# Borders between the stages of a two-layer encoder: who adds the residual and splits the activations, and in what order the last gated-linear head finishes

## Chip, cores and metric

The kernel runs on one core of a Trainium2 chip. The metric is the device time of one execution, in microseconds (us); lower is better.

## What is computed

The reference runs 1024 prompt frames and 64 frames of a running stream (T = 1088 tokens together, D = 1024 channels, all in float32) through two layers:

```
layer 1: x += rms_norm(gated_linear_attention(rms_norm(x))) ; x += rms_norm(mlp(rms_norm(x)))
layer 2: x += rms_norm(sliding_window_attention(rms_norm(x))) ; x += rms_norm(mlp(rms_norm(x)))
rms_norm(x) = x / sqrt(mean(x * x) + 1e-6) * g        mlp(h) = relu(h @ w_up) ** 2 @ w_down
gated linear, per head, chunks of 64 frames: scores = (q decayed) @ (k decayed).T ; out = q @ state + scores @ v
        state = decay * state + k.T @ v ; out = rms_norm(out) * g * silu(r) ; result = out @ w_out
```

## The kernel before

**Layout.** Activations lie transposed: channels on the 128 partitions (eight tiles `k` or `m` of 128 channels), tokens along the free axis, in three blocks `b` of 384, 384 and 320 tokens. float32 accuracy comes from splitting each operand in a high and a low part: `h_hi`, `h_lo` for activations and `w_hi`, `w_lo` for weights, and three matmul passes (hi x hi, lo x hi, hi x lo).

**Weights.** They come in 180 units of 128 x 1024 values (512 KB) through four slots. SP's queue loads `w_raw`, ScalarE casts it to `w_hi` (`high` of the stream, L151), GpSimd subtracts and writes `w_lo` (L158), and TensorE's last matmul of a unit frees the slot. `dense` and `dense_set` (L181, L201) are the matmuls of a unit.

**Stages.** Gated linear (4 heads), MLP, attention, MLP. Each stage ends with a last wave, whose positions are (b, q): block b, output tile q, about one output tile of 12 to 24 matmuls each, and starts with a first wave, whose positions are (b, j): block b, output group j. Between two stages stands a `Border`; the program calls it five times (before the first stage, three in the middle, after the last). Its steps, for each block:

- the norm of the stage's output: `square` (ScalarE, L381) squares each tile, `add_squares` (VectorE, L463) adds it to an accumulator, `sums` (TensorE, L314) adds over partitions, `inverse` (VectorE and ScalarE's `root`) makes 1/sqrt and a diagonal (L512, L515), `spread` (TensorE, L323) spreads it over the partitions into a bank, and `scale` (VectorE, L524) multiplies the tiles `y`;
- the residual: `load_x` brings the old x from DRAM through four slots (`X_SLOTS`), `add_x` (L533) adds it;
- the next stage's input: `high` (ScalarE, L407) writes `h_hi` with the next norm's gain and squares x (L412), `low` (VectorE, L548) writes `h_lo`; `add_squares_x` (L477), `sums_x` (L333), `inverse_x`, `spread_x` (L340) and `keep_block` (ScalarE, L419) make that norm's factor, which is applied after the next stage's first matmuls, so the first wave doesn't wait for it before its results are taken.

The order on each engine is written out by hand: `tensor_in_last_wave`, `tensor_in_first_wave`, `scalar_...`, `vector_...` say at which position which step is issued. `step(b, s)` on VectorE issues `scale` of tile s with the steps that follow it for earlier tiles. Block 0 is normed within the last wave, block 1 around its end, block 2 in the first wave of the next stage. In the last border the same steps end in the output: `high` only asks for the next residual, and the tail is stored by SP.

**Gated linear.** Each head runs nine pairs p of chunks; a pair has three slots (`PARTS`), and a planner puts jobs (projections of the next head, for head 3 the first parts of the output projection) into `STEPS` slots, from which TensorE fills the time in which the pair's chain runs: turned key, scores (L1868), attention (VectorE, L2390), state update (L1906, L2415), output (L1922, L1925). `HIGHS` says at which slot ScalarE casts which weight unit. In head 3, `silu`, `early_high` (L2106) and `early_low` (L2313) prepare the gated outputs of earlier heads, `end_early` issues the four early jobs of the output projection, `gated` (L2299) finishes head 3's own outputs, and turn_rows (L1812) turns them.

## Time and profile before

| | |
|---|---|
| median of three executions | 2671.1 us (2668.15 to 2671.66) |
| the profiled execution | 2670.47 us, span 2668.7 us |
| mean granted TensorE clock | 0.971 of full speed |
| busy | TensorE 2531.0 us (95%), VectorE 967.9 (36%), ScalarE 822.0 (31%), GpSimd 445.0 (17%) |
| DMA | 139 MB, mean 52 GB/s |

The span is what the profiler covers of one execution; the execution's own time is 1.8 us more. Busy times are sums over the whole span, so they don't say where an engine waits. PE is TensorE, DVE VectorE, ACT ScalarE, POOL GpSimd, PEld TensorE's weight loads; L323 is line 323 of the kernel before. The granted clock is given in parts of full speed, 2.4 GHz.

### The profile page before, as it was taken

The page shows a single profiled execution, that of the slowest core. Times are in us where ns is not written, and L with a number is a line of the kernel's source. Part 1 is how long each engine was busy: PE and PEld are TensorE (multiplying, and loading weights), DVE is VectorE, ACT ScalarE, POOL GpSimd, SP SyncE. Part 2 cuts the span into 40 slices and gives each one's busy share as a digit, 9 for nine tenths or more (in the row PEclk, how much of TensorE's full clock was granted, in tenths as well). Part 3 has the DMA queues.
Part 4 walks back from the last instruction along what each step waited for, and adds up shares of the span by engine and source line. Part 5 has one row for each costly group of instructions (what it writes and reads, how often), then busy time and mean ns, then how long its engine had stood idle before and what let it go on. Part 6 is the DMA issues. An engine that isn't in the chain of part 4 may idle for free.

```text
span 2668.7 us, 41573 instructions
## 1 busy us (share of the span) xinstructions
PE 2531.0 (95%) x17454; PEld 2388.1 (89%) x17454; DVE 967.9 (36%) x1913; ACT 822.0 (31%) x1618; POOL 445.0 (17%) x186
## 2 busy tenths in 40 slices
PE   6999999898999999999998999889899999999997
PEld 5778878698999999999997977688899999999996
DVE  6354454416422222222228344425522222222227
ACT  4445444335311211120224355535411211211221
POOL 1101110111112211212211010112112212211210
PEclk9999999899999999999999999999999999999998
DMA  3101010013211111111113200103311111111113
GB/s 106 41 9 47 25 39 26 29 48 114 80 40 48 44 42 47 39 47 39 57 42 119 80 25 18 37 25 98 95 48 40 47 39 47 42 44 47 39 60 123
DMA packets 63088, 139.05 MB, mean 52 GB/s; under 512 B 8688, under 2 KB 39920, under 8 KB 62960
## 3 DMA queue, kind: packets, MB, share of 16 engines
q1 hardware_dynamic: 33984, 103.60, 12.0%
q10 hardware_dynamic: 28976, 33.64, 4.1%
q8 instruction: 93, 1.52, 0.2%
q14 instruction: 35, 0.29, 0.0%
HBM read 117.81 MB, written 19.40 MB: 51 GB/s over the span
## 4 chain that ended last, share of the span: by engine, by line
PE 77%; DVE 5%; issue 2%; ACT 2%; ACTq 0%; DMA 0%; DVEq 0%; SPq 0%
PE banks L201 51%; PE banks L181 19%; PE banks L1769 1%; DVE h_lo L548 1%; DVE norm_acc_x L477 1%; DVE norm_acc L463 1%; DVE y L524 1%; PE banks L1269 1%; PE banks L1288 1%; PE banks L323 0%; PE banks L1256 0%; PE banks L1296 0%; PE banks L1922 0%; PE banks L1925 0%; ACT y L1422 0%
## 5 line engine op out<-in xcount | busy, mean ns | idle before, releaser
L158 POOL TENSOR_TENSOR w_lo<-w_raw,w_hi 128x1024 fp32r<-128x1024 f32 x180 | 443.4, 2467 | 2151.3 <-ACT w_hi L151 2151.3
L181 PE MATMUL banks<-h_hi,w_hi 128*128 128x384 f32 (+1 forms) x1224 | 437.9, 358 | 8.1 <-POOL w_lo L158 5.3
L181 PE MATMUL banks<-h_lo,w_hi 128*128 128x384 f32 (+1 forms) x1224 | 415.9, 340 | 0.0
L181 PE MATMUL banks<-h_hi,w_lo 128*128 128x384 f32 (+1 forms) x1224 | 414.5, 339 | 0.0
L151 ACT CAST w_hi<-w_raw 128x1024 fp32r<-128x1024 f32 x180 | 187.0, 1047 | 468.0 <-DMA w_raw<-in_units 467.1
L201 PE MATMUL banks<-h_hi,w_hi 128*128 128x384 f32 (+1 forms) x1368 | 301.7, 329 | 0.0
L201 PE MATMUL banks<-h_hi,w_lo 128*128 128x384 f32 (+1 forms) x1368 | 301.3, 328 | 0.0
L201 PE MATMUL banks<-h_lo,w_hi 128*128 128x384 f32 (+1 forms) x1368 | 301.3, 328 | 0.0
L201 PE MATMUL banks<-mlp_a_hi,w_hi 128*128 128x384 f32 (+1 forms) x1344 | 296.6, 329 | 1.5 <-issue 1.3
L201 PE MATMUL banks<-mlp_a_lo,w_hi 128*128 128x384 f32 (+1 forms) x1344 | 295.1, 327 | 0.0
L201 PE MATMUL banks<-mlp_a_hi,w_lo 128*128 128x384 f32 (+1 forms) x1344 | 295.0, 327 | 0.0
L987 DVE TENSOR_TENSOR y<-banks,y 128x768 f32<-128x768 f32 x192 | 130.1, 719 | 401.6 <-PE banks L201 400.1
L916 ACT ACTIVATE mlp_act<-mlp_act 128x1088 f32<-128x1088 f32 x56 | 62.5, 1115 | 656.3 <-DVE mlp_act L973 656.3
L181 PEld LDWEIGHTS banks<-h_hi,w_hi 128*128 128x128 f32 x1224 | 241.5, 197 | 21.8 <-issue 19.0
L181 PEld LDWEIGHTS banks<-h_lo,w_hi 128*128 128x128 f32 x1224 | 241.8, 198 | 2.2 <-issue 0.6
L181 PEld LDWEIGHTS banks<-h_hi,w_lo 128*128 128x128 f32 x1224 | 240.9, 197 | 0.0
L973 DVE SCALAR_TENSOR_TENSOR mlp_act<-banks,keep 128x768 f32<-128x768 f32 x112 | 75.9, 720 | 444.5 <-PE banks L201 444.5
L201 PEld LDWEIGHTS banks<-h_hi,w_hi 128*128 128x128 f32 x1368 | 233.8, 188 | 0.0
L201 PEld LDWEIGHTS banks<-h_hi,w_lo 128*128 128x128 f32 x1368 | 233.8, 188 | 0.0
L201 PEld LDWEIGHTS banks<-h_lo,w_hi 128*128 128x128 f32 x1368 | 233.8, 188 | 0.0
L201 PEld LDWEIGHTS banks<-mlp_a_hi,w_hi 128*128 128x128 f32 x1344 | 226.7, 188 | 5.5 <-DVE y L987 3.1
L201 PEld LDWEIGHTS banks<-mlp_a_lo,w_hi 128*128 128x128 f32 x1344 | 227.3, 188 | 0.0
(191 smaller groups left out, 3108.3 us busy)
## 6 DMA issues: line engine op xcount, KB each, us to landing
w_raw<-in_units SPq DMA_DIRECT2D x180, 512.0 KB, 3.5
x_scratch<-y ACTq DMA_DIRECT2D x48, 192.0 KB, 2.5
norm_x<-x_scratch ACTq DMA_DIRECT2D x48, 192.0 KB, 3.3
x_scratch<-y ACTq DMA_DIRECT2D x24, 160.0 KB, 1.8
norm_x<-x_scratch ACTq DMA_DIRECT2D x24, 160.0 KB, 3.1
y<-in_x SPq DMA_DIRECT2D x16, 192.0 KB, 4.7
norm_x<-in_x ACTq DMA_DIRECT2D x16, 192.0 KB, 3.5
out_y<-y SPq DMA_DIRECT2D x16, 192.0 KB, 2.7
```

Source lines behind the costliest of these rows:

```text
L151: self.chip.nc.scalar.copy(self.chip.w_hi[:, s], self.chip.w_raw[:, s]).then_inc(self.hi_done, 1)
L158: c.nc.gpsimd.tensor_tensor(c.w_lo[:, s], c.w_raw[:, s], c.w_hi[:, s].bitcast(F32), ALU.subtract).then_inc(self.ready, 1)
L181: mm = chip.nc.tensor.matmul(out, w, x, start=(first and n == 0), stop=(last and n == 2))
L201: mm = chip.nc.tensor.matmul(chip.banks[:, 3 * s + b, 0:WIDTH[b]], w, x[:, k, COLS[b]], start=(k == 0 and n == 0), stop=(k == n_k - 1 and ...
L463: self.chip.nc.vector.tensor_tensor(self.s.acc[:, 0:n], before, self.s.sq[:, m % 2, 0:n], ALU.add).then_inc(self.s.summed, 1)
L477: self.chip.nc.vector.tensor_tensor(self.s.acc_x[:, 0:n], before, self.s.sq_x[:, k % 2, 0:n], ALU.add).then_inc(self.s.summed_x, 1)
L524: self.chip.nc.vector.scalar_tensor_tensor(out=y, in0=y, scalar=self.chip.gains[:, gain, k:k + 1], in1=self.chip.banks[:, RS_BANK + b % 2, ...
L548: op = nc.vector.scalar_tensor_tensor(out=lo, in0=y, scalar=self.chip.gains[:, self.pre, k:k + 1], in1=hi.bitcast(F32), op0=ALU.mult, op1= ...
L916: nc.scalar.activation(self.act[:, j % 2], self.act[:, j % 2], ACT.Square).then_inc(self.squared, 1)
L973: op = nc.vector.scalar_tensor_tensor(out=out, in0=bank, scalar=0.0, in1=keep, op0=ALU.max, op1=ALU.mult)
L987: op = nc.vector.tensor_tensor(y, bank, y, ALU.add)
L1269: nc.tensor.transpose(out[:, 0:P], prob[:, 1:1 + P], chip.ident[:])
```

## The change

At the middle borders and the last one:

- ScalarE's squares go to a bank (`SQ_BANK`, `SQ_X_BANK`) instead of SBUF, the first of a block straight into the accumulator, which has two halves. The matmuls `sums` and `sums_x` write their column sums to the bank that the spread factor takes later, so the separate banks for them go.
- GpSimd adds the residual and makes the low parts of block 0 and of the even tiles of blocks 1 and 2. For these ScalarE first writes the scaled tile to SBUF (`gained`), waits for it, and casts it to `h_hi`; GpSimd subtracts. The odd tiles of blocks 1 and 2 stay with VectorE. In the last border half of block 2's additions stay there too.
- VectorE makes the low parts of the first four weight units of the three later stages (`first_low`), which were GpSimd's.
- The norm matmuls stand at other places of the last and the first wave, and with them the steps of ScalarE and VectorE.

In the gated-linear stage: in head 0 the cast of weight unit 4 stands ahead of the first level exponent; in head 3 the jobs are planned over 21 slots instead of 18, all four early jobs come after the last pair, `silu` and the first `early_high` move behind ScalarE's part of pair 7's turned key, the second to pair 8, and `early_low` one place later each, the last one behind the first gated outputs.

```diff
-SUM_BANK, RS_BANK, KEEP_BANK = 4, 5, 7
+SQ_BANK, RS_BANK, SQ_X_BANK = 4, 5, 7
...
+    def first_low(self, dve, unit):
+        c, s = self.chip, unit % SLOTS
+        dve.wait_ge(self.hi_done, unit + 1)
+        c.nc.vector.tensor_tensor(c.w_lo[:, s], c.w_raw[:, s], c.w_hi[:, s].bitcast(F32),
+                                  ALU.subtract).then_inc(self.first_ready, 1)
...
+    def low_by_vector(self, b, k):
+        return self.first or (b > 0 and k % 2 == 1)
+    def gained(self, b, k):
+        n = self.added * (NB * KT - KT) + self.count_alike(b, k)
+        return n, self.s.sq[:, n % 2, 0:WIDTH[b]]
...
     def sums(self, pe, b):
         pe.wait_ge(self.s.summed, self.per_norm(KT - 1) + (KT - 1) * (b + 1))
-        if b:
-            pe.wait_ge(self.s.var_done, self.per_norm(1) + b)
+        if b == 2:
+            self.bank_left(pe)
         for j, t in enumerate(self.TILES[b]):
-            mm = self.chip.nc.tensor.matmul(self.chip.banks[:, SUM_BANK, j:j + 1], self.s.acc[:, t:t + P],
-                                            self.chip.ones[:, 0:1], start=(j == 0), stop=(j == 2))
+            mm = self.chip.nc.tensor.matmul(self.chip.banks[:, RS_BANK + b % 2, j:j + 1],
+                                            self.s.acc[:, b % 2, t:t + P], self.chip.ones[:, 0:1],
+                                            start=(j == 0), stop=(j == 2))
         mm.then_inc(self.s.sum_full, 1)
+    def bank_left(self, pe):
+        if self.middle:
+            pe.wait_ge(self.s.kept, self.per_pre(1) + 1)
+        else:
+            pe.wait_ge(self.s.scaled, self.per_norm(KT) + KT)
...
     def spread(self, pe, b):
         pe.wait_ge(self.s.diag_done, self.per_norm(1) + b + 1)
-        if b == 2:
-            pe.wait_ge(self.s.scaled, self.per_norm(KT) + KT)
...
-        if (b, q) == ((2, 1) if self.last else (2, 4)):
+        if (b, q) == (2, 1):
             self.sums(pe, 1)
-        if (b, q) == ((2, 3) if self.last else (2, 7)):
+        if (b, q) == (2, 3):
             self.spread(pe, 1)
-        if (b, q) == (2, 7) and self.middle:
+    def tensor_in_first_wave(self, pe, b, j):
+        if (b, j) == (0, 0):
             self.sums_x(pe, 0)
-    def tensor_in_first_wave(self, pe, b, j):
-        if (b, j) == (0, 0):
+        if (b, j) == (0, 1):
             self.spread_x(pe, 0)
+        if (b, j) == (0, 2):
             self.sums(pe, 2)
-        if (b, j) == (0, 2):
+        if (b, j) == (0, 3):
             self.spread(pe, 2)
-        if (b, j) == (0, 3):
+        if (b, j) == (1, 0):
             self.sums_x(pe, 1)
-        if (b, j) == (1, 0):
+        if (b, j) == (1, 1):
...
+        at += max(m - 2, min(m - 1, 1)) if self.first else max(m - 1, 0)
         if at > 0:
             act.wait_ge(self.s.summed, at)
-        self.chip.nc.scalar.activation(self.s.sq[:, m % 2, 0:WIDTH[b]], self.chip.y[:, m, COLS[b]],
-                                       ACT.Square).then_inc(self.s.squared, 1)
+        out = self.s.sq[:, m % 2, 0:n] if self.first else self.chip.banks[:, SQ_BANK, 0:n]
+        if m == 0 and not self.first:
+            act.wait_ge(self.s.sum_full, self.per_norm(1) + b // 2)
+            out = self.s.acc[:, b % 2, 0:n]
+        self.chip.nc.scalar.activation(out, self.chip.y[:, m, COLS[b]], ACT.Square).then_inc(self.s.squared, 1)
...
-        nc.scalar.activation(self.chip.h_hi[:, k, COLS[b]], y, ACT.Copy,
-                             scale=self.chip.gains[:, self.pre, k:k + 1]).then_inc(self.s.hi_done, 1)
-        at = self.per_pre(KT - 1) + (KT - 1) * b + max(k - 2, min(k - 1, 1))
+        hi, gain = self.chip.h_hi[:, k, COLS[b]], self.chip.gains[:, self.pre, k:k + 1]
+        if self.low_by_vector(b, k):
+            nc.scalar.activation(hi, y, ACT.Copy, scale=gain).then_inc(self.s.hi_done, 1)
+        else:
+            n, gained = self.gained(b, k)
+            if n > 2:
+                act.wait_ge(self.s.lo_done, n - 2)
+            nc.scalar.activation(gained, y, ACT.Copy, scale=gain).then_inc(self.s.gained, 1)
+            act.wait_ge(self.s.gained, n)
+            nc.scalar.copy(hi, gained).then_inc(self.s.hi_done, 1)
+        at, n = self.per_pre(KT - 1) + (KT - 1) * b + max(k - 1, 0), WIDTH[b]
         if at > 0:
             act.wait_ge(self.s.summed_x, at)
-        nc.scalar.activation(self.s.sq_x[:, k % 2, 0:WIDTH[b]], y, ACT.Square).then_inc(self.s.squared_x, 1)
+        out = self.chip.banks[:, SQ_X_BANK, 0:n]
...
+        nc.scalar.activation(out, y, ACT.Square).then_inc(self.s.squared_x, 1)
...
-        if (b, q) == ((2, 2) if self.last else (2, 6)):
+        if (b, q) == (2, 2):
             self.root(act, 1)
-        if b == 1 and q >= 5:
-            self.high(act, 0, q - 5)
+        if b == 1 and q >= 4:
+            self.high(act, 0, q - 4)
...
-        elif b == 2 and q < 5:
-            self.high(act, 0, q + 3)
+            if b == 2 and q < 2:
+                self.high(act, 0, 2 * q + 4)
+                self.high(act, 0, 2 * q + 5)
+            if b == 2 and q >= 5:
+                self.high(act, 1, 2 * q - 10)
+                self.high(act, 1, 2 * q - 9)
+        elif b == 2 and q < 4:
+            self.high(act, 0, q + 4)
...
+    def x_by_vector(self, b, k):
+        return self.last and b == NB - 1 and k % 2 == 1
...
+            op = ops.tensor_tensor(lo, self.gained(b, k)[1], hi.bitcast(F32), ALU.subtract)
+        op.then_inc(done, 1)
+    def gpsimd(self, pool):
+        ops = self.chip.nc.gpsimd
+        for b in range(NB):
+            for k in range(KT + 1):
+                if k < KT and not self.x_by_vector(b, k):
+                    self.add_x(pool, ops, b, k, self.s.x_new)
+                if self.middle and k and not self.low_by_vector(b, k - 1):
+                    self.low(pool, ops, b, k - 1, self.s.lo_done)
     def step(self, dve, b, s):
+        ops = self.chip.nc.vector
         if s < KT:
             self.scale(dve, b, s)
         if self.first:
             if s >= 2:
-                self.low(dve, b, s - 2)
-            return
-        if 1 <= s <= KT:
-            self.add_x(dve, b, s - 1)
-        if self.middle and s >= 3:
-            self.low(dve, b, s - 3)
-        if self.middle and s >= 4:
-            self.add_squares_x(dve, b, s - 3)
+                self.low(dve, ops, b, s - 2, self.s.lo_done_v)
+        elif self.middle:
+            if 3 <= s <= KT + 1:
+                self.add_squares_x(dve, b, s - 2)
+            if b and s >= 3 and self.low_by_vector(b, s - 3):
+                self.low(dve, ops, b, s - 3, self.s.lo_done_v)
+        elif s >= 1 and self.x_by_vector(b, s - 1):
+            self.add_x(dve, ops, b, s - 1, self.s.x_new_v)
...
-            if b == 2 and q < 6:
-                self.step(dve, 0, q + 5)
-            if (b, q) == (2, 6):
-                self.inverse(dve, 1)
-            if (b, q) == (2, 7):
-                self.step(dve, 1, 0)
...
+        elif b == 2:
+            self.step(dve, q // 5, (q + 5) % (2 * 5))
+            if q == 4:
+                self.chip.stream.first_low(dve, self.next_unit)
+            if q == 6:
+                self.chip.stream.first_low(dve, self.next_unit + 1)
+        if (b, q) == (2, 2):
+            self.inverse(dve, 1)
...
         ws.high(act, next_unit + 2)
+        self.high(act, 1, 0)
+        ws.high(act, next_unit + 3)
+        self.high(act, 1, 1)
         self.root_x(act, 0)
-        self.high(act, 1, 0)
-        self.high(act, 1, 1)
-        ws.high(act, next_unit + 3)
+        self.high(act, 1, 2)
+        self.high(act, 1, 3)
         self.keep_block(act, 0)
     def scalar_in_first_wave(self, act, b, j):
-        if (b, j) == (0, 1):
+        if b == 0:
+            for k in ((4, 5), (6,), (7,), ())[j]:
+                self.high(act, 1, k)
+        if (b, j) == (0, 2):
             self.root(act, 2)
         if (b, j) == (0, 3):
+            for k in range(3):
+                self.high(act, 2, k)
             self.root_x(act, 1)
+            self.high(act, 2, 3)
+            self.high(act, 2, 4)
+            self.keep_block(act, 1)
+        if b == 1:
+            for k in ((5, 6), (7,), (), ())[j]:
+                self.high(act, 2, k)
         if (b, j) == (1, 3):
             self.root_x(act, 2)
...
     def vector_before_first_wave(self, dve):
         self.add_squares(dve, 2, KT - 1)
+        self.chip.stream.first_low(dve, self.next_unit + 2)
+        self.step(dve, 1, 3)
+        self.chip.stream.first_low(dve, self.next_unit + 3)
         self.inverse_x(dve, 0)
-        self.steps(dve, 1, 1, 4)
+        self.steps(dve, 1, 4, 6)
     def vector_in_first_wave(self, dve, b, j):
         if (b, j) == (0, 0):
-            self.steps(dve, 1, 4, 7)
+            self.steps(dve, 1, 6, 8)
         if (b, j) == (0, 1):
-            self.steps(dve, 1, 7, 9)
-            self.inverse(dve, 2)
+            self.step(dve, 1, 8)
         if (b, j) == (0, 2):
             self.steps(dve, 1, 9, 11)
+            self.inverse(dve, 2)
         if (b, j) == (0, 3):
+            self.steps(dve, 2, 0, 5)
             self.inverse_x(dve, 1)
-            self.steps(dve, 2, 0, 2)
-        if b == 1 and j < 3:
-            self.steps(dve, 2, 3 * j + 2, 3 * j + 5)
+            self.steps(dve, 2, 5, 7)
+        if b == 1 and j < 2:
+            self.step(dve, 2, 7 + j)
+        if (b, j) == (1, 2):
+            self.steps(dve, 2, 9, 11)
...
     def scalar_after_all(self, act):
-        for k in range(4, KT):
+        for k in range(6, KT):
...
-    STEPS = (PARTS * NPAIR, PARTS * NPAIR, PARTS * NPAIR, 18)
+    STEPS = (PARTS * NPAIR, PARTS * NPAIR, PARTS * NPAIR, 21)
     GATE_AT = (1, 3, 3)
     HIGHS = ({2: 6, 4: 7, 10: 8, 15: 9}, {4: 4, 6: 5, 10: 6, 13: 7, 16: 8, 19: 9}, {4: 4, 6: 5, 10: 6, 13: 7, 16: 8, 19: 9},
-             {4: 4, 6: 5, 11: 6, 13: 7, 16: 8, 21: 9})
-    FILL_AT = (23, 25)
...
-        for m in range(len(self.FILL_AT), JOB_BANKS):
+        for m in range(JOB_BANKS):
...
+        ws.high(act, 4)
         level_exp(0)
         copy_value(7)
         level_exp(1)
-        ws.high(act, 4)
+        ws.high(act, 5)
         copy_value(8)
-        ws.high(act, 5)
...
+                if h == GH - 1 and p == 7:
+                    silu(h)
+                    early_high(0)
+                if h == GH - 1 and p == 8:
+                    early_high(1)
...
-                if h == GH - 1 and p in (6, 7):
-                    early_low(p - 6)
+                if h == GH - 1 and p == 7:
+                    early_low(0)
         output_variance(GH)
         output_inverse(GH)
-        early_low(2)
+        early_low(1)
         for j in range(NB):
             gated(GH - 1, 2 * j)
             gated(GH - 1, 2 * j + 1)
             if j:
                 low_parts(j - 1)
+            if j == 1:
+                early_low(2)
...
```

## Rows read from the trace of the kernel before

**Rows 1.** Busy time of each engine, and the DMA issues of the weight units.
```profile
PE 2531.0 (95%) x17454; PEld 2388.1 (89%) x17454; DVE 967.9 (36%) x1913; ACT 822.0 (31%) x1618; POOL 445.0 (17%) x186
...
w_raw<-in_units SPq DMA_DIRECT2D x180, 512.0 KB, 3.5
```

**Rows 2.** TensorE's waits, whole span: total us, times, longest us.
```profile
PE banks L323 <- DVE norm_diag L512: 21.3, 7, 6.8
...
PE banks L181 <- POOL w_lo L158: 5.3, 1, 5.3
```

**Rows 3.** Windows: us, busy (instructions) by engine, granted clock, DMA share, GB/s.
```profile
638.70:714.30 75.60, 63.13 (x323) 60.61 (x322) 51.61 (x108) 36.51 (x73) 13.38 (x6) 0.84 0.33 106
1437.20:1511.00 73.80, 60.47 (x326) 57.89 (x325) 50.63 (x104) 32.11 (x64) 12.71 (x5) 0.88 0.35 114
1850.20:1924.20 74.00, 62.29 (x322) 59.70 (x322) 50.76 (x107) 36.16 (x73) 13.72 (x6) 0.86 0.33 107
...
644.30:651.90 7.60, 7.54 (x24) 6.94 (x25) 5.96 (x12) 3.02 (x7) 4.99 (x2) 0.51 0.21 73
667.30:672.40 5.10, 5.02 (x15) 4.63 (x16) 3.04 (x7) 2.08 (x5) 0.00 (x0) 0.51 0.43 131
695.70:703.20 7.50, 7.42 (x31) 7.42 (x32) 1.89 (x7) 1.14 (x3) 0.00 (x0) 0.54 0.00 1
570.00:609.80 39.80, 39.80 (x243) 39.80 (x242) 4.13 (x7) 12.38 (x23) 9.59 (x4) 1.00 0.17 54
2641.20:2646.00 4.80, 4.74 (x30) 4.48 (x31) 3.45 (x9) 0.94 (x2) 0.00 (x0) 1.00 0.43 126
```

**Rows 4.** TensorE's waits from 540 to 727 us, around the first middle border.
```profile
PE banks L323 <- DVE norm_diag L512: 5.6, 1, 5.6
PE banks L323 <- DVE norm_diag L515: 4.0, 1, 4.0
...
PE banks L333 <- DVE norm_acc_x L477: 2.9, 1, 2.9
```

**Rows 5.** Timeline at 640 us, GpSimd and VectorE: start us, us, instruction, idle before.
```profile
640.09 2.76 POOL L158 TENSOR_TENSOR w_lo<-w_raw,w_hi 128x1024 fp32r<-128x1024 f32 x1 [41.47 <-ACT w_hi L151]
...
640.10 0.55 DVE L477 TENSOR_TENSOR norm_acc_x<-norm_acc_x,norm_sq_x 128x384 f32<-128x384 f32 x1
640.74 2.46 DVE L463 TENSOR_TENSOR norm_acc<-norm_acc,norm_sq 128x320 f32<-128x320 f32 x1
```

**Rows 6.** GpSimd's groups: instruction, shapes, count; busy us, mean ns; idle before, releaser.
```profile
L158 POOL TENSOR_TENSOR w_lo<-w_raw,w_hi 128x1024 fp32r<-128x1024 f32 x180 | 443.4, 2467 | 2151.3 <-ACT w_hi L151 2151.3
L2468 POOL TENSOR_TENSOR gla_rank_w<-gla_rank_w,all_ones 128x128 fp32r<-128x128 f32 x1 | 0.7, 674 | 9.7 <-DMA gla_rank_w<-in_gate_a 9.7
```

**Rows 7.** Groups of ScalarE and of VectorE from 605 to 715 us.
```profile
L407 ACT ACTIVATE h_hi<-y,gains 128x384 fp32r<-128x384 f32 x16 | 9.8, 611 | 3.8 <-DVE y L533 3.4 <-issue 0.3
L412 ACT ACTIVATE norm_sq_x<-y 128x384 f32<-128x384 f32 x16 | 8.2, 515 | 1.2 <-DVE norm_acc_x L477 1.2
...
L907 ACT CAST mlp_a_hi<-mlp_act 128x384 fp32r<-128x384 f32 x8 | 4.1, 513 | 0.3
...
L533 DVE TENSOR_TENSOR y<-y,norm_x 128x384 f32<-128x384 f32 x16 | 9.3, 580 | 0.0
```

**Rows 8.** Windows in the gated-linear stage.
```profile
98.10:107.50 9.40, 4.09 (x14) 3.91 (x13) 2.05 (x2) 5.33 (x10) 4.67 (x2) 0.54 0.18 56
499.60:551.00 51.40, 34.71 (x244) 25.43 (x242) 19.65 (x37) 21.04 (x35) 3.24 (x2) 0.75 0.05 16
```

**Rows 9.** Timeline of ScalarE: the end of the chunk decays, and a weight cast.
```profile
94.67 0.23 ACT L2043 ACTIVATE gla_end_decay<-gla_b 128x17 f32<-128x17 f32 x1 [1.91 <-DVE gla_b L2335]
...
525.00 1.04 ACT L151 CAST w_hi<-w_raw 128x1024 fp32r<-128x1024 f32 x1 [11.06 <-DMA w_raw<-in_units]
```

**Rows 10.** Timeline of VectorE: an early low part, and the last residual addition.
```profile
513.82 2.56 DVE L2313 TENSOR_TENSOR h_lo<-y,h_hi 128x2304 fp32r<-128x2304 f32 x1 [7.96 <-ACT h_hi L2106]
...
2665.98 0.49 DVE L533 TENSOR_TENSOR y<-y,norm_x 128x320 f32<-128x320 f32 x1 [0.84 <-DMA norm_x<-x_scratch]
```

More of the change, by code:

```diff
@@ L1023, in gpsimd @@
             ws.low(pool, u0 + 8 * (FF_GROUPS - 1) + i)
+        if self.after.last:
+            self.after.gpsimd(pool)
 class Swa(EndWave):
@@ L1846, in fill @@
                 job_step(job, k)
-            if h == GH - 1 and slot in self.FILL_AT:
-                end_early(self.FILL_AT.index(slot))
         def end_early(m):
```

139 lines of the change are left out of this document (68 added, 71 removed).

## The prediction

> **What bounds the kernel now.** I read the head of the page first. TensorE is busy for 95% of the span [rows 1], so a change pays only where TensorE waits, or where it runs at the lower clock. The profiled execution took 2670.5 us, 0.6 us under the median of the three runs, and my sums are made against it.
>
> The list of TensorE's waits came next. The longest are waits for the diagonal that carries a norm's factor, 21.3 us over the kernel from one line of it; one wait of 5.3 us is for the low part of a weight unit [rows 2]. Then I cut the trace by stretches, each running from the end of a stage's last matmul to the end of the next stage's first wave. The three middle borders take 75.6, 73.8 and 74.0 us at a granted clock of 0.84 to 0.88 [rows 3]. In the first, TensorE waits 5.6 + 4.0 + 2.9 = 12.5 us [rows 4]. After each wait the clock stands near 1.2 GHz (0.51 to 0.54) for 7.6, 5.1 and 7.5 us [rows 3], which loses 0.49 x 7.6 + 0.49 x 5.1 + 0.46 x 7.5 = 9.7 us. So 22.2 us of this border are lost and 53.4 us are work at the full clock. The same work in the others leaves 20.4 and 20.6 us, and the three borders lose 63.2 us: the most that this part can return. The fourth border shows the other side: after a wait of about 1 us at 2641 the clock stayed at 1.00 [rows 3].
>
> Two stretches of the gated-linear stage lose time too. From 98.1 to 107.5 us TensorE worked for 4.1 us of 9.4. From 499.6 to 551.0, the last three chunk pairs and the turns of the last head, it was busy for 34.7 us of 51.4, at a mean clock of 0.75 [rows 8].
>
> **Head 0: `high(4)` ahead of the level exponents.** The chunk decays end at 94.9; a cast of 1.04 us [rows 9] and a GpSimd subtraction of 2.47 us [rows 6] bring the low part at 98.4, where TensorE arrives at 98.1. The wait of 5.3 us goes, and the 4 us at half clock behind it (2 us). Not all 7.3 us are kept: the first scores also need the last value copy, which now stands behind a second cast (1.04 us). I take **5.5 us**, bounds 3 and 7.3.
>
> **Last head.** Jobs spread over 21 slots instead of 18 fill pair 6, and all four early output jobs come behind the loop. Today ScalarE runs silu and an h_hi cast before pair 7's turned key, VectorE's 2.56 us of `early_low(0)` stands in front of pair 7's attention, and ScalarE waits 11.06 us for a weight unit before it takes pair 7's output [rows 9, 10]. The change moves each of these past that place. The weight unit is now asked for only with the first early job, so output 8 is taken some 5 us late, but the early jobs (72 matmuls x 0.164 us from the full-clock row [rows 3] = 12 us) cover it. Moving `early_low(2)` behind the gates frees the turns.
>
> TensorE's own work in the 51.4 us: 12 us of early jobs, about 3.5 us for each of three pairs, 4 us of turns: 27 us. So idle is 16.7 and low clock about 7.7. I leave 7.2 of idle (pairs 7 and 8 still chain scores, attention, output; the earlier pairs have less cover) and 3.3 of low clock: **14 us** gained, bounds 7 (the chain of 7 and 8 stays as long as now) and 18.
>
> **Middle borders: what goes.** VectorE loses 24 residual additions (0.58 us each [rows 7]) and 16 low parts (about as much) per border, gets four weight low parts, about 1.1 us each (VectorE's 2.56 us for 2304 elements scaled by 1024), and its square sums read one operand from a bank. The second accumulator half takes the wait for `sum_full` away, so `sums(1)` and `spread(1)` move from (2, 4) and (2, 7) to (2, 1) and (2, 3), and block 1 is scaled two steps earlier. The wait of 5.6 us at the end of the last wave stood on that chain. Also, four unit subtractions leave GpSimd, and the low parts are ready when units have landed.
>
> **What comes.** GpSimd has no row for 384 columns. A line through its rows (0.67 us at 128, 2.47 at 1024) [rows 6] gives 1.19 us, 1.06 at 320. Bounds: 0.93 (the large row pro rata) and 2.47 (never above the larger row). The kernel's smaller shape lies nearer 128, so I take the line. Block 0 has 16 such operations, 19 us, blocks 1 and 2 twelve each, 14.3 and 12.7: 46 us of 75. Block 0's first scale follows `spread(0)` at (1, 3), so half of block 1's jobs and all of block 2's are still to run: 144 matmuls x 0.164 = 23.6 us. The 19 us are covered.
>
> ScalarE is tighter. A `high` is now scaled copy 0.61, wait on itself, cast 0.51, square 0.52 [rows 7]: some 1.65 us against 1.0 to 1.1. With the wave's own square and half a take it needs about 2.3 us per step, and TensorE's step is 12 matmuls, 2.1 us in block 1 and 1.76 in block 2. Over the steps from (1, 4) to (2, 2) it falls 2 to 3 us behind; `root(1)` stands behind this queue and behind VectorE's wait for the squares of x. `spread(1)` then comes about 2.3 us after TensorE is there, inside the last wave. With a low clock between none (after 1 us) and 3.5 (after 2.9) I charge 1.5.
>
> In the first wave, measured from the last wave's end E: unit 3 lands at E+4 (its slot is used to the last matmul; landing takes 3.5 us [rows 1]), its cast ends at E+5, and `root_x(0)`, `high(1,2)`, `high(1,3)` and `keep_block(0)` follow by E+10. From there ScalarE has eight activation casts and squares and four heavy `high`s before `root(2)`: the diagonal is ready at about E+22.4, TensorE reaches `spread(2)` at E+18.9. So a wait of 3.5 us stays, with 2.6 of low clock. `sums_x(2)` and `spread_x(1)` are nearly free: 1 us together.
>
> Reads of two SBUF tensors on VectorE wait while GpSimd works: a square sum took 2.46 us where its neighbour took 0.55, ending 0.35 us behind a GpSimd subtraction [rows 5]. The change keeps such reads (eight low parts, six diagonals, four unit low parts, twelve activation low parts in the dense stages) while GpSimd is busy 46 of 75 us; only those on the path count, 1 us.
>
> The Trainium skill, "SBUF — State Buffer", section "Who interferes with whom", says that a VectorE instruction with two SBUF inputs and a GpSimd instruction that reads SBUF exclude each other for a whole instruction. The trace agrees at 640.7. By that rule 30 reads meet a busy GpSimd 0.6 of the time for half an instruction, some 11 us of VectorE per border; if all of it lay on the path, a border would return nothing.
>
> The borders keep 2.3 + 1.5 + 3.5 + 2.6 + 1 + 1 = 11.9 us of loss (11.4 before the attention stage, whose takes cost one ScalarE operation instead of two), and return 10.3, 9 and 8.7: **28 us**.
>
> The "GPSIMD Engine Reference" of the Trainium skill, section "3.1 Elementwise — side-by-side cycle accounting", measures 4.50 us for 2048 elements; pro rata that estimates 0.84 us for 384. GpSimd would be lighter still, the sum the same, since ScalarE sets it.
>
> **Last border.** The tail waits for residual loads that follow the additions [rows 10]. Half the last block's additions go to GpSimd (1.06 us against 0.49 [rows 10]), the block-1 additions leave the path of `inverse(2)`, but `root(2)` stands behind `high(1,7)` and so behind GpSimd's eighth addition. Gain **1 us**, between -3 and 4.
>
> **Sum.** 5.5 + 14 + 28 + 1 = 48.5; 2670.5 - 48.5 = 2622, I write 2621.
>
> **Rivals.** (B) The borders close almost wholly: ScalarE issues its pairs back to back and the roots come in time. For it: VectorE is freed by more than it is given. Against it: the queue order above. A loss of 2 us per border stays: 57 + 20.5 = 77.7 us, 2593. (C) GpSimd's length, its exclusion with VectorE and ScalarE's longer queue put new waits where the old ones were; the borders return nothing. For it: rows 5. Only the gated-linear parts and the tail stay: 2650. (D) The other side: GpSimd becomes the bound. It has 40 operations per border; when 40p passes 75.6 + 7 us, that is p above 2.06 us, each border loses 7 us more than now and the 20.5 us are used up. At the bound of 2.47 a border takes 99 us, 24 more: 2670.5 - 20.5 + 3 x 24 = 2722. Against it: 0.67 us at 128. (E) It changes nothing: the heads give 7 and the borders lose as much by waits behind GpSimd. 2670.
>
> **Chances.** Mine 0.50 (its own range 2605 to 2638: POOL's price, ScalarE's lag, and the last head giving 7 to 18), B 0.20, C 0.20, D 0.06, E 0.04. The range 2588 to 2655 reaches into B and C and leaves out a quarter of B, some of C, D and E. A change within 0.2% (5 us) can't be told from none here. Faster 0.90, same 0.04, slower 0.06.
>
> **What would show it.** The w_lo wait of 5.3 us is gone; GpSimd's 384-column operations near 1.2 us; the window from 499.6 on some 14 us shorter; middle borders of about 65 us, with a wait at `spread(1)` inside the last wave and one at `spread(2)`. Wrong would be: ScalarE's self-wait much longer than 0.1 us, operations of 2 us on GpSimd, or TensorE held by h_lo of block 0 at the start of a stage.

## The result, and the profile after

The changed kernel took 2627.3 us (median; 2623.4 to 2632.5 in four executions) against 2671.4 before: ratio 0.9836, 95% interval 0.9814 to 0.9857, a gain of 44 us. The prediction was 2621 us, range 2588 to 2655, so the time lies inside its likeliest case. The profiled execution took 2626.1 us.

Busy times of the engines after; they answer to [rows 1]:

```profile
PE 2509.7 (96%) x17454; PEld 2370.0 (90%) x17454; DVE 910.4 (35%) x1785; ACT 842.0 (32%) x1666; POOL 554.4 (21%) x314
```

TensorE does the same 17454 matmuls. VectorE loses 58 us of work, GpSimd gains 109, ScalarE 20.

TensorE's waits of the whole span after (total us, times, longest):

```profile
PE banks L369 <- DVE norm_diag L580: 22.8, 5, 6.7
...
PE banks L369 <- DVE norm_diag L577: 7.5, 7, 1.6
...
PE banks L385 <- DVE norm_diag_x L577: 4.8, 3, 2.8
...
PE banks L197 <- ACT gla_v_tok L2110: 3.0, 1, 3.0
```

L369 is `spread`, L385 `spread_x`. The diagonal that ended the waits of 5.6 to 6.8 us at `spread(1)` [rows 2, 4] now costs 1.5 us; the one of `spread(2)` has grown from 4 to 6.7 us in the first border and is the longest wait of a border (the wait for the first block at the start of the execution is longer, 11.9 us, and was 12.1 before). The wait for a weight's low part in head 0 is gone, and a wait of 3.0 us for a value copy stands there.

Windows after: the three middle borders (from the end of the last wave to the end of the first), then the stretches behind `spread(2)` in the first and the second border, behind `spread_x(0)` in the second, and behind `spread(1)` in the first:

```profile
617.90:682.30 64.40, 56.27 (x322) 54.30 (x320) 37.54 (x77) 37.23 (x77) 26.22 (x26) 0.92 0.35 112
1407.68:1474.30 66.62, 58.96 (x323) 56.90 (x322) 33.95 (x71) 32.10 (x66) 25.73 (x25) 0.90 0.35 111
1816.97:1880.45 63.48, 56.19 (x321) 54.22 (x320) 37.25 (x76) 36.50 (x76) 25.40 (x25) 0.92 0.36 113
...
645.40:653.00 7.60, 7.60 (x29) 7.20 (x29) 3.99 (x9) 4.69 (x10) 4.78 (x6) 0.63 0.29 89
1437.50:1445.00 7.50, 7.50 (x29) 7.10 (x29) 3.42 (x8) 4.26 (x9) 4.72 (x6) 0.64 0.28 88
1420.70:1427.60 6.90, 6.90 (x28) 6.59 (x26) 3.87 (x8) 3.52 (x8) 3.20 (x4) 0.63 0.49 149
...
610.10:613.10 3.00, 3.00 (x18) 2.73 (x19) 1.85 (x4) 2.37 (x6) 1.80 (x2) 1.00 0.72 183
```

They answer to the first three of [rows 3], 75.6, 73.8 and 74.0 us. Behind the waits of 6.7, 4.8 and 2.8 us the granted clock stands at 0.63 to 0.64 over 7 us, behind the one of 1.5 us it stays at 1.00.

Two windows of the gated-linear stage, cut at the same instructions in both kernels: head 0 from the spread of block 2 to the output that waits for its second state, and the last head from its first scores to its last turn. First the kernel before, then the changed one:

```profile
55.43:125.64 70.21, 63.88 (x475) 56.44 (x475) 29.73 (x69) 27.17 (x51) 7.07 (x3) 0.93 0.11 33
446.24:550.95 104.71, 88.02 (x768) 70.84 (x768) 48.69 (x112) 43.74 (x87) 14.28 (x6) 0.86 0.10 33
```

```profile
54.91:122.41 67.50, 63.44 (x475) 56.02 (x475) 31.28 (x69) 27.12 (x51) 9.34 (x3) 0.95 0.11 35
438.70:528.80 90.10, 84.65 (x773) 69.24 (x773) 47.57 (x110) 43.49 (x87) 14.26 (x6) 0.92 0.12 38
```

The last head is 14.6 us shorter, head 0 2.7 us. Heads 1 and 2, which no edit touches, are 4.5 us shorter together (116.0 + 99.2 us before, 113.0 + 97.7 after).

GpSimd's groups after, to be read beside [rows 6]:

```profile
L604 POOL TENSOR_TENSOR y<-y,norm_x 128x384 f32<-128x384 f32 x64 | 66.1, 1043 | 100.4 <-DVE y L589 99.2 <-DMA norm_x<-x_scratch 1.0
L626 POOL TENSOR_TENSOR h_lo<-norm_sq,h_hi 128x384 fp32r<-128x384 f32 x36 | 36.6, 1017 | 43.2 <-ACT h_hi L466 39.5 <-DVE y L589 3.5
```

### The profile page after: what moved, and what is told of

It reads as the page before. It is cut to its first block, busy times and chain, and to the rows that moved or that the text cites. A ratio compares the mean times of both kernels' runs of the same rounds, so it can differ in the third digit from the quotient of the medians.

```text
span 2624.3 us, 41637 instructions
## 1 busy us (share of the span) xinstructions
PE 2509.7 (96%) x17454; PEld 2370.0 (90%) x17454; DVE 910.4 (35%) x1785; ACT 842.0 (32%) x1666; POOL 554.4 (21%) x314
## 3 DMA queue, kind: packets, MB, share of 16 engines
q1 hardware_dynamic: 33984, 103.60, 12.1%
## 4 chain that ended last, share of the span: by engine, by line
PE 78%; ACT 3%; DVE 3%; issue 2%; ACTq 1%; DMA 0%; POOL 0%; DVEq 0%; POOLq 0%
PE banks L217 52%; PE banks L197 18%; PE banks L1860 1%; PE banks L1380 1%; PE banks L1361 1%; ACTq L339 1%; ACT norm_sq L464 1%; PE banks L1348 1%; PE banks L1388 0%; DVE norm_acc_x L542 0%; PE banks L2011 0%; PE banks L369 0%; PE banks L2014 0%; PE banks L1995 0%; ACT w_hi L153 0%
## 5 line engine op out<-in xcount | busy, mean ns | idle before, releaser
L160 POOL TENSOR_TENSOR w_lo<-w_raw,w_hi 128x1024 fp32r<-128x1024 f32 x168 | 414.9, 2473 | 1870.1 <-ACT w_hi L153 1870.1
L197 PEld LDWEIGHTS banks<-h_hi,w_hi 128*128 128x128 f32 x1224 | 236.5, 193 | 20.5 <-issue 12.6
```

Source lines behind the costliest of these rows:

```text
L160: c.nc.gpsimd.tensor_tensor(c.w_lo[:, s], c.w_raw[:, s], c.w_hi[:, s].bitcast(F32), ALU.subtract).then_inc(self.ready, 1)
L197: mm = chip.nc.tensor.matmul(out, w, x, start=(first and n == 0), stop=(last and n == 2))
```

## The experiments

To compare borders between kernels I cut each trace at the same TensorE instructions into four stretches: the first border with the wave before it, the second and the third from their `spread(0)` or the end of the attention's main part on, and the tail. For the changed kernel:

```profile
534.40:682.95 148.55, 138.31 (x817) 135.57 (x817) 60.06 (x121) 73.67 (x153) 53.17 (x46) 0.97 0.30 97
1381.24:1514.58 133.34, 119.80 (x775) 111.24 (x775) 68.52 (x147) 68.31 (x166) 49.37 (x44) 0.95 0.32 103
1723.61:1881.08 157.47, 148.10 (x888) 144.84 (x889) 60.47 (x122) 79.12 (x158) 53.15 (x46) 0.97 0.28 89
2579.37:2613.82 34.45, 27.26 (x162) 25.18 (x162) 21.88 (x49) 6.38 (x15) 15.91 (x16) 0.95 0.57 180
sum 473.81, PE 433.48 PEld 416.83 DVE 210.94 ACT 227.48 POOL 171.61; mean PE 108.37 PEld 104.21 DVE 52.73 ACT 56.87 POOL 42.90
```

All runs, with the median in us, the ratio to the kernel before with its interval, and these stretches:

| run | median | ratio (95%) | border 1 | 2 | 3 | tail | sum |
|---|---|---|---|---|---|---|---|
| kernel before | 2671.4 | 1 | 157.5 | 138.0 | 166.2 | 35.0 | 496.7 |
| changed kernel | 2627.3 | 0.9836 (0.9814-0.9857) | 148.6 | 133.3 | 157.5 | 34.5 | 473.8 |
| gla_only | 2647.8 | 0.9910 (0.9893-0.9926) | 156.8 | 137.7 | 166.7 | 35.0 | 496.1 |
| last_head_only | 2658.5 | 0.9951 (0.9935-0.9968) | 156.9 | 137.8 | 166.3 | 35.0 | 495.9 |
| old_queue_order | 2635.1 | 0.9867 (0.9842-0.9892) | 147.5 | 133.2 | 157.4 | 33.9 | 472.0 |
| adds_on_vector | 2635.7 | 0.9871 (0.9854-0.9887) | 149.4 | 140.3 | 158.4 | 34.2 | 482.4 |
| squares_sbuf | 2647.4 | 0.9924 (0.9897-0.9951) | 152.8 | 140.9 | 163.4 | 35.7 | 492.8 |
| sbuf_and_adds_on_vector | 2646.4 | 0.9905 (0.9889-0.9922) | 152.5 | 141.4 | 162.1 | 36.4 | 492.3 |
| gpsimd_doubled | 2681.4 | 1.0034 (1.0021-1.0046) | 165.3 | 151.2 | 179.7 | 34.1 | 530.3 |
| inverse2_early | 2618.9 | 0.9809 (0.9793-0.9826) | 144.3 | 131.3 | 154.3 | 33.7 | 463.6 |
| all_early | 2621.6 | 0.9813 (0.9792-0.9834) | 146.0 | 133.0 | 155.9 | 34.1 | 469.0 |
| inv2_block1_vector | 2621.1 | 0.9809 (0.9785-0.9834) | 146.9 | 132.3 | 155.9 | 34.1 | 469.2 |
| inv2_high_first | 2622.8 | 0.9819 (0.9793-0.9845) | 146.8 | 132.1 | 155.0 | 34.0 | 468.0 |
| best | 2626.5 | 0.9833 (0.9808-0.9857) | 147.3 | 132.3 | 158.1 | 34.2 | 471.8 |

The medians are of four to six executions; the stretches are read from one execution of each kernel. Kernels with the same borders show what that is worth: 495.9 to 496.7 us for the three with the borders of before, 473.8 and 472.0 for the changed kernel and old_queue_order. A difference of some 2 us in a sum says nothing.

**Which part gives what: gla_only and last_head_only.** The first puts only the gated-linear edits of the change's diff on the kernel before. The second starts from the first and puts head 0 back as it was:

```diff
-        ws.high(act, 4)
         level_exp(0)
         copy_value(7)
         level_exp(1)
+        ws.high(act, 4)
+        copy_value(8)
         ws.high(act, 5)
-        copy_value(8)
```

> The kernel before with the gated-linear edits alone (cast of unit 4 ahead in head 0; last head rearranged); the borders as before. My sum: 5.5 + 14 = 19.5 us less than before, 2651; by the stretches of the changed kernel's trace 3.0 + 15.5 = 18.5, 2652. If the 4.6 us that heads 1 and 2 also lost there belong to these edits, 2647.5, and the same stretches must be short here too. Rival C (borders return nothing, all comes from here): 2627.

> The kernel before with the edits of the last head alone; head 0 and the borders as before. The run with both gated-linear edits took 2647.8 us, and its trace shows head 0 shorter by 2.7, head 1 by 3.0, head 2 by 1.5 to 3, the last head by 14.7 us. Heads 1 and 2 are not edited; before, a stretch at low clock stood behind a wait of 0.9 us there. Theory (head 0's edit moves the phase in which that clock drop falls): heads 1 and 2 are as long as before, 2671.4 - 14.7 = 2656 to 2657. Rival (the drop is chance of one execution): they are short here too, 2650 to 2652.

gla_only came out at 2647.8: 23.6 us from the gated-linear edits, 20.5 from the borders. The border stretches are as long as before (496.1 against 496.7 us), so the two halves don't touch each other. last_head_only gave 12.7 us by the medians, and heads 1 and 2 were as long as before: 116.1 + 99.2 us, against 113.1 + 96.1 in gla_only. Head 0 itself differs by 2.2 us between the two (69.8 and 67.6). Head 0's edit thus went with 6.1 us in heads 1 and 2, which it doesn't touch. In the window behind the same wait of 0.9 us in head 1, for last_head_only and for gla_only:

```profile
229.60:246.00 16.40, 16.37 (x112) 12.63 (x112) 6.31 (x19) 5.21 (x11) 2.37 (x1) 0.79 0.19 59
```

```profile
229.60:246.00 16.40, 16.20 (x130) 13.32 (x130) 9.23 (x26) 7.32 (x16) 2.38 (x1) 1.00 0.21 61
```

112 matmuls against 130, at a clock of 0.79 against 1.00. It is a clock drop, not work. In fourteen profiled executions it stands in four: before, last_head_only, best, and sbuf_and_adds_on_vector, whose head 0 is edited as in the changed kernel. The same wait of 0.9 us at the start of head 2 shows it too: a low clock stands behind it in these four and, for a shorter time, in the changed kernel and in inverse2_early, where head 2 took 97.7 us, against 96.2 in the eight executions without one. So the edit makes the drop rarer at most, and what decides stays open.

**The last head's queue order: old_queue_order.** The changed kernel, with `silu`, `early_high` and `early_low` at their places of before, the jobs as changed:

```diff
-                if h == GH - 1 and p == 7:
+                if h == GH - 1 and p == 6:
                     silu(h)
                     early_high(0)
-                if h == GH - 1 and p == 8:
+                if h == GH - 1 and p == 7:
                     early_high(1)
```

> The changed kernel with ScalarE's and VectorE's order of the last head as before (silu and the early casts behind pairs 6 and 7, the early low parts behind pairs 6, 7 and the loop), but jobs over 21 slots and all early jobs behind the loop. Theory (the order carries a good part: before, pair 7's turned key waited 3.3 us and the state 2.6 behind these operations): 4 to 8 us slower than the changed kernel, 2631 to 2635, by waits of 2 to 3 us in pairs 7 and 8. Rival (the jobs' places carry the 14.7 us): within 2 us of 2627.

2635.1, 7.8 us slower, at the upper edge of the theory's range. The last head's window, cut as above, shows more:

```profile
437.96:538.95 100.99, 87.38 (x772) 70.10 (x773) 49.45 (x111) 43.33 (x87) 14.24 (x6) 0.88 0.11 34
```

It took 101.0 us, against 90.1 in the changed kernel and 104.7 before. So the order carries 10.9 us of the 14.6 in these executions, about three quarters; in the total, borders and heads 1 and 2 that came out 3.4 us shorter in this execution hide a part of it. No run has the new order with the old places of the jobs, so what the jobs' places give by themselves isn't shown. TensorE's longest waits from 480 to 545 us in this run:

```profile
PE banks L1995 <- ACT gla_kdt L2202: 5.3, 2, 4.8
PE banks L2011 <- DVE gla_state L2504: 2.5, 1, 2.5
```

They are the waits of before at the same steps, pair 7's turned key behind `silu` and the state behind `early_low(0)`.

**Additions and squares: adds_on_vector, squares_sbuf, sbuf_and_adds_on_vector.** In the first, GpSimd's additions of the middle borders go back to VectorE; in the second, the squares go to one SBUF buffer per norm (the kernel before had two per norm); the third does both:

```diff
         elif self.middle:
+            if 1 <= s <= KT:
+                self.add_x(dve, ops, b, s - 1, self.s.x_new)
...
-            before, square = acc, self.chip.banks[:, SQ_BANK, 0:n]
+            before, square = acc, self.s.one[:, 0:n]
```

> The changed kernel with the residual additions of the three middle borders back on VectorE, at step s for tile s-1 as before; GpSimd keeps the low parts. Theory (VectorE's relief carries the border's gain): 24 additions of 0.58 us come back per border, the additions for block 0 stand in front of inverse(1), the wait at spread(1) grows from 1.5 to 4 or more and a low clock follows: 4 to 6 us per border, 2640 to 2645. Rival (the new places and the second accumulator half carry it): within 3 us of 2627. Rival (GpSimd's additions are themselves the cost, by their length of 1.04 us and by holding VectorE): faster than 2622.

> The changed kernel with the squares of both norms written to one buffer each in SBUF instead of a bank, same order and same waits, so that VectorE's additions of squares read two SBUF tensors. Theory (only reads on the path count, about 1 us per border): 0 to 3 us per border, 2627 to 2636. Rival (VectorE and GpSimd exclude each other for a whole operation): 45 additions per border meet a busy GpSimd half the time and wait half of 1.04 us, 12 us of VectorE per border, and the means of the additions rise from 0.55 to 0.8 us; if half lies on the path, 18 us in all, 2645.

> The changed kernel with the squares in SBUF and the residual additions of the middle borders on VectorE, so that GpSimd has 16 low parts per border and no additions. Squares in SBUF alone cost 20.1 us, additions on VectorE alone 8.4. Theory (VectorE's additions of two SBUF tensors wait for GpSimd's operations, one by one): GpSimd has less than half of its operations left, so the squares in SBUF cost at most half of 20 here: 2640 to 2646, below the run with GpSimd adding, and the mean of the 384-column additions of squares falls from 0.87 to 0.65 us or less. Rival (squares in SBUF are slow by themselves, or by ScalarE): the two costs add, 2656.

With the borders of gla_only at 496.1 us as the base, the four sums of the table make a square: squares in SBUF return 3.3 us with GpSimd adding and 3.8 with VectorE adding; squares in a bank return 13.7 with VectorE adding and 22.3 with GpSimd adding. So handing the additions to GpSimd is worth nothing (-0.5 us) while the squares are in SBUF, and 8.6 us once they are in a bank; the bank itself is worth 10 to 19 us against one SBUF buffer per norm. Against the two buffers of before it wasn't run, and it may be worth less there. The medians say the same: 8.4 us for the additions with the bank, 10.7 and 20.1 us for the bank. GpSimd keeps the 16 low parts in all four kernels, so what those are worth isn't shown.

My theory for squares_sbuf fell (0 to 9 us expected, 20.1 measured, its four executions from 2643.4 to 2659.3); its rival stood at 18. The theory for adds_on_vector came short, and its reason was wrong: the wait at `spread(1)` of the first border did not grow (1.3 us), the one at `spread(2)` did, from 6.7 to 8.6 us there and from 4.8 to 8.0 us in the second border. Borders 1 and 3 lost only 0.9 us each, border 2 lost 7.0. The third run lay 9.9 us over adds_on_vector in the border stretches, as its theory said; its total also holds the clock drop of heads 1 and 2, and the mean of its additions fell less than I expected (below).

How it comes about: VectorE's additions of the next norm's squares, whole span, in the changed kernel, in squares_sbuf and in sbuf_and_adds_on_vector:

```profile
L542 DVE TENSOR_TENSOR norm_acc_x<-norm_acc_x,banks 128x384 f32<-128x384 f32 x42 | 23.2, 552 | 30.8 <-ACT banks L475 30.5
```

```profile
L543 DVE TENSOR_TENSOR norm_acc_x<-norm_acc_x,norm_one_x 128x384 f32<-128x384 f32 x42 | 35.8, 853 | 26.9 <-ACT norm_one_x L476 26.8
```

```profile
L543 DVE TENSOR_TENSOR norm_acc_x<-norm_acc_x,norm_one_x 128x384 f32<-128x384 f32 x42 | 33.3, 792 | 20.0 <-ACT norm_one_x L476 20.0
```

552 ns from a bank, 853 from SBUF with 40 GpSimd operations per border, 792 with 16. Taken one by one, the third kernel's 42 additions fall into two groups: the 26 that start while GpSimd is idle take 0.55 us (0.549 in the mean), the 16 that start during a GpSimd operation 1.03 to 1.39 us. In squares_sbuf 32 of the 42 start during one, with 0.95 us in the mean. So fewer GpSimd operations meet fewer additions, but in the third kernel each meeting costs more, and the mean hardly falls. The kernel before settles the rival that SBUF is slow by itself: its additions (L477) read two SBUF tensors, and 39 of 42 ran with GpSimd idle, in 0.55 us. In the changed kernel 38 of 42 start during a GpSimd operation and still take 0.55. One addition in squares_sbuf (start us, us), and one in the changed kernel beside two GpSimd additions:

```profile
628.39 1.01 POOL L627 TENSOR_TENSOR h_lo<-norm_sq,h_hi 128x384 fp32r<-128x384 f32 x1 [2.98 <-ACT h_hi L467]
...
628.77 1.04 DVE L543 TENSOR_TENSOR norm_acc_x<-norm_acc_x,norm_one_x 128x384 f32<-128x384 f32 x1 [0.18 <-ACT norm_one_x L476]
```

```profile
629.86 2.32 POOL L604 TENSOR_TENSOR y<-y,norm_x 128x384 f32<-128x384 f32 x2
...
630.77 0.55 DVE L542 TENSOR_TENSOR norm_acc_x<-norm_acc_x,banks 128x384 f32<-128x384 f32 x1
```

The SBUF addition starts inside a GpSimd operation and ends 0.41 us behind it, after 1.04 us; the one with a bank operand runs under GpSimd in 0.55.

**How far GpSimd is from being the bound: gpsimd_doubled.** A second operation of the same size, into a spare buffer, ahead of each GpSimd addition and low part of the middle borders, each of which also waits for the one before it:

```diff
+            self.again(engine, ops, self.s.x[:, k % self.X_SLOTS, 0:WIDTH[b]], self.s.x[:, k % self.X_SLOTS, 0:WIDTH[b]])
         ops.tensor_tensor(y, y, self.s.x[:, k % self.X_SLOTS, 0:WIDTH[b]], ALU.add).then_inc(done, 1)
```

> The changed kernel with a second GpSimd operation of the same size ahead of each residual addition and each low part of the middle borders (its result goes to a spare buffer), so that GpSimd's price per operation is about 2.08 us instead of 1.04. This is the point at which rival D of the prediction decides: 40 operations x 2.08 = 83 us per border against 64 to 67 now. Theory (GpSimd then bounds the border): middle borders of 80 to 85 us, total 2670 to 2685. Rival (GpSimd's gaps take it in, since it is busy 42 of 64 us now and its operations for block 0 are covered): below 2645.

2681.4 us, as the theory said, and slower than before. TensorE's waits from 530 to 700 us:

```profile
PE banks L370 <- DVE norm_diag L578: 12.7, 1, 12.7
PE banks L370 <- DVE norm_diag L581: 8.8, 1, 8.8
```

`spread(1)` waits 12.7 us instead of 1.5: block 0's operations, which stand on the way to it, run out of cover first. The 120 added operations took 109 us (four groups: 42.9 + 36.5 + 18.5 + 11.1) and cost 54 us of time. By a straight line, which is an estimate, the 44 us of gain are used up after 109 x 44 / 54 / 120 = 0.74 us more per operation, at about 1.75 us. The added operations read SBUF too, so a part of the 54 us can be VectorE's waiting for them; the run doesn't part the two.

**The wait at spread(2): inverse2_early, all_early, inv2_block1_vector, inv2_high_first, best.** In the changed kernel, `sums(2)` ends at 634.3 and TensorE reaches `spread(2)` at 638.7, but the diagonal is done at 645.3. ScalarE's and VectorE's timelines there:

```profile
641.10 0.52 ACT L995 ACTIVATE mlp_act<-mlp_act 128x384 f32<-128x384 f32 x1 [1.62 <-DVE mlp_act L1048]
...
642.07 0.61 ACT L459 ACTIVATE h_hi<-y,gains 128x384 fp32r<-128x384 f32 x1
...
644.28 0.20 ACT L436 ACTIVATE rs<-var 128x3 f32<-128x3 f32 x1 [1.22 <-DVE var L549]
...
643.10 0.55 DVE L542 TENSOR_TENSOR norm_acc_x<-norm_acc_x,banks 128x384 f32<-128x384 f32 x1 [1.56 <-ACT banks L475]
643.57 0.61 DVE L623 SCALAR_TENSOR_TENSOR h_lo<-y,gains,h_hi 128x384 fp32r<-128x384 f32 x1
644.10 0.15 DVE L549 TENSOR_SCALAR var<-banks 128x3 f32<-128x3 f32 x1
```

`var` of block 2 stands on VectorE behind the last steps of block 1, and these behind ScalarE's `high(1, 7)`, 10 us after the sums were there. inverse2_early moves the two:

```diff
         if (b, j) == (0, 0):
             self.steps(dve, 1, 6, 8)
+            self.inverse(dve, 2)
...
         if (b, j) == (0, 2):
             self.steps(dve, 1, 9, 11)
-            self.inverse(dve, 2)
```

and `root(2)` behind `high(1, 5)`. all_early also has `inverse(1)` ahead of VectorE's step at (2, 2) and `inverse_x(0)` ahead of the fourth unit's low part. inv2_block1_vector and inv2_high_first stand on inverse2_early:

```diff
-        return self.first or (b > 0 and k % 2 == 1)
+        return self.first or b == 1 or (b == 2 and k % 2 == 1)
...
-        ws.high(act, next_unit + 2)
         self.high(act, 1, 0)
-        ws.high(act, next_unit + 3)
+        ws.high(act, next_unit + 2)
         self.high(act, 1, 1)
+        ws.high(act, next_unit + 3)
```

best takes these two and inverse2_early together, and swaps `ws.high(act, 5)` and `copy_value(8)` in head 0.

> The changed kernel with inverse(2) on VectorE right behind steps (1, 6) and (1, 7) of the first wave's position (0, 0), and root(2) on ScalarE behind high(1, 5), instead of behind the last steps of block 1 at (0, 2). Theory (the 6.7 us wait at spread(2) is the order of the two queues, not their length): the wait falls to 1 us or less and the low clock behind it goes, 7 to 10 us per border; the next thing that can be late is the low part of (1, 7). 2600 to 2608. Rival (VectorE and ScalarE are full, the work is only shifted): the wait moves to the low parts of block 1 or to the next norm matmuls, total within 6 us of 2627.

> The changed kernel with inverse(2) early as in the run before, and also inverse(1) ahead of VectorE's step at (2, 2), and inverse_x(0) ahead of the low part of the fourth weight unit. Theory (each norm matmul waits for a diagonal that stands behind unrelated work): the waits of 1.5 at spread(1) and 0.5 to 2.8 at spread_x(0) go as well, 1.5 to 3 us per border below 2619: 2611 to 2615. Rival (ScalarE's queue up to high(1, 7) sets the end of block 1 anyway, so what is gained ahead of it is waited for at the low part of (1, 7), 2.3 us now): 2617 to 2620, with that wait longer by as much.

> The run with inverse(2) early (2618.9 us), and all eight low parts of block 1 on VectorE instead of four, so that ScalarE casts four tiles fewer per border and GpSimd subtracts four fewer. Theory (ScalarE's queue up to high(1, 7) sets the end of block 1): each of the four saves 0.5 us of ScalarE, the wait of 2.3 us at the low part of (1, 7) falls below 1 us and the low clock behind it goes: 1.5 to 4 us per border, 2607 to 2614. Rival (VectorE is as full as ScalarE, and it takes 0.6 us for each): 2617 or more.

> The run with inverse(2) early (2618.9 us), and high(1, 0) and high(1, 1) on ScalarE each one place ahead, before the casts of the third and the fourth weight unit, which wait for their transfers. Theory (as for the run with block 1 on VectorE, by another lever: ScalarE stands idle for 1.4 us there): 0.5 to 1.5 us per border, 2614 to 2617. Rival (the two go in by the same transfer anyway): 2618 to 2620.

> The changed kernel with inverse(2) early, block 1's low parts on VectorE, high(1, 0) and high(1, 1) one place ahead, and in head 0 the last value copy ahead of the cast of unit 5. Theory: the border parts as in the two runs beside it, together 2605 to 2612; head 0's wait of 3.05 us, which ends with the value copy behind a cast of 1.04 us, falls to 2.0, another 1 us and some low clock: 2603 to 2611. Rival (another engine's queue sets the same waits): above 2615.

inverse2_early is the fastest of all by its median, 8.3 us less than the changed kernel (2614.9 to 2624.2 against 2623.4 to 2632.5), with 10.2 us less in the border stretches. That is a third to half of what I expected and more than the rival allowed. Its waits from 530 to 700 us, and the window behind the new one:

```profile
PE banks L197 <- DVE h_lo L623: 2.3, 1, 2.3
PE banks L369 <- DVE norm_diag L577: 1.5, 1, 1.5
...
PE banks L385 <- DVE norm_diag_x L577: 0.5, 1, 0.5
```

```profile
645.20:649.00 3.80, 3.79 (x14) 3.79 (x15) 2.72 (x6) 2.42 (x5) 1.98 (x3) 0.50 0.00 0
```

The 6.7 us are gone and 2.3 us for the low part of (1, 7) stand in their place, with a clock of 0.50 behind them: theory and rival each had half. The other runs tested what sets that low part, and my theory of ScalarE's queue fell: with four casts fewer the wait was 2.8 us, and 1.0 us came back at `spread(2)`; with `high(1, 0)` ahead it was 2.3, and `spread_x` waited 4.6 us in two places instead of 0.5. None of the four came below inverse2_early. Their border stretches were 4.4 to 8.2 us longer, but inverse2_early's profiled execution was its fastest, 4 us under its median; by the medians all_early, inv2_block1_vector and inv2_high_first are 2.2 to 3.8 us slower, and the executions overlap, so that these three are worse isn't shown. all_early's rival was near in the time (2621.6 against 2617 to 2620) but not in the place: `spread(1)` waited 0.7 us less, and 0.7 us more came back at the low parts, 0.8 us at `spread(2)` and 2.3 us at `spread_x`, where the rival had all of it at the low part of (1, 7). In best, head 0's wait fell from 3.05 to 2.11 us as expected, and the clock drop made heads 1 and 2 4.5 us longer than in inverse2_early or the changed kernel (116.0 + 99.2 us). In the timeline of inverse2_early ScalarE and VectorE both stand idle for 1.5 to 2.1 us in each position, each waiting for the other (take, cast, `high`, addition, next take), so I now take the place of `high(1, 7)`, one position behind `high(1, 6)`, for the cause. It wasn't tried, so this isn't shown.

## Why the prediction was right, point by point

**The sum.** 48.5 us were forecast: 5.5 + 14 + 28 + 1 (the prediction writes 2621 where this gives 2622). Cut at the same instructions, the traces show 2.7 in head 0, 14.6 in the last head, 22.3 in the middle borders and 0.6 in the tail, 40.2 in all, and 4.5 in heads 1 and 2, against 44.4 between the two spans. So a tenth of the gain is luck: it comes from a clock drop that the prediction didn't know of. Without it the time would be near 2632, still within the likeliest case. Head 0 and the borders were each forecast too high.

**Last head.** 14 us forecast, 14.6 in the stretch, 12.7 by the run alone. The reason given, ScalarE's and VectorE's operations ahead of pair 7, is shown by old_queue_order, which loses 10.9 us in this stretch and 7.8 in the total.

**Head 0.** 5.5 forecast, 2.7 in its stretch. The step that was mis-sized is the last value copy behind the second cast: I charged about the cast's 1.04 us, and TensorE waited 3.0 us for it with the clock low behind. What made good for it, 4.5 us in heads 1 and 2 (6.1 in gla_only), I hadn't foreseen, and it is a clock drop that comes and goes.

**Borders.** 28 us forecast in the middle, 21.8 measured against gla_only: 8.2, 4.4 and 9.2 where I had 10.3, 9 and 8.7. The likeliest case had the right mechanism for the waits: `spread(1)` moved inside the last wave and waited 1.5 us (forecast 2.3) without a low clock (1.5), and `spread(2)` kept a wait. That one was mis-sized: 6.7 us and 0.37 x 7.6 = 2.8 of low clock, against 3.5 + 2.6. I had the queue before `root(2)` right but took it as work; it was mostly the order. In border 2 the wait at `spread_x(0)` took 2.8 us and 0.37 x 6.9 = 2.6 of clock, and my sum had no term for it: its 1 us is for `sums_x(2)` and `spread_x(1)`. That is the miss there: of these 5.4 us a loss at `spread(1)` smaller than forecast made some up, and 4.6 us remain.

**GpSimd.** 1.19 us forecast from the line through two rows, 1.04 measured. The estimate that the prediction worked out from the "GPSIMD Engine Reference" of the Trainium skill, section "3.1 Elementwise — side-by-side cycle accounting", was 0.84 and lay below it. The unit's low part on VectorE took 1.25 us (forecast 1.1). Rival D needed 2.06 us for the gain of the borders to be gone; in gpsimd_doubled, where an operation and its double took 1.9 us in the mean, the kernel was already 10 us slower than before, and the straight line has it break even near 1.75. So D was put too far off.

**What I credited wrongly.** My text took VectorE's relief, 24 additions and 16 low parts, for the source of the gain, and gave the squares in a bank no price. The square of runs shows another picture: the bank is worth 10 to 19 us (against one SBUF buffer) and the additions' relief 8.6 at most, and without the bank the rest returns 3 to 4 us. The relief by the 16 low parts and the new places of the norm matmuls stay unparted. I had weighed the exclusion of two-input SBUF reads and GpSimd from "SBUF — State Buffer" of the Trainium skill, section "Who interferes with whom", only for the 30 reads that the change keeps, at 1 us per border on the path. The runs agree with that rule (in sbuf_and_adds_on_vector 1.03 to 1.39 us for the additions that start during a GpSimd operation and 0.55 for the others; 0.55 with one operand in a bank), and the change mostly escapes it: in squares_sbuf 42 reads more per border cost 4.2, 7.6 and 5.9 us.

**Last border.** 1 us forecast, 0.5 measured. **Rival C** (the borders return nothing) is nearly what happens in squares_sbuf, whose borders return 3.3 us: right mechanism, but the bank takes its condition away.

## What to carry to other kernels

Before work goes to GpSimd, look at what VectorE reads while GpSimd runs: operands in a bank make the hand-over of the additions worth 8.6 us here, the same operands in SBUF make it worth nothing. Where an engine waits long for a small result (a root, a diagonal), look when its input was ready: 10 us of queue order can stand between, and moving it shows the next link at about half the gain. Cut both traces at the same instructions before crediting a change; 4.5 us of this gain lay in stretches that the change doesn't edit.

## What the runs showed of the hardware

A VectorE addition of two SBUF tensors of 384 columns took 0.55 us while GpSimd was idle and 1.03 to 1.39 us where it started during a GpSimd operation (sbuf_and_adds_on_vector); with one operand in a bank it took 0.55 either way. At the borders the granted clock fell to 0.50 to 0.64 behind waits of 2.3 us and more and stayed at 1.00 behind one of 1.5 us. The length of a wait alone doesn't decide it: in the changed kernel's last head a wait of 1.6 us ended at 506.5 us, and from 507.7 to 514.5 the clock was 0.50. Behind the same wait of 0.9 us in head 1 it stood at 0.79 in one kernel and at 1.00 in another. This moved the time of heads 1 and 2 by 6 us with the same instructions in them.
